# One of three gathered blocks' second-table rows weighed and added by GpSimd, and the gathers dealt out anew

## The chip, the cores and the metric

The kernel runs on one core of a Trainium2 chip. Its engines are TensorE (PE), VectorE (DVE), ScalarE (ACT), GpSimd (POOL) and SyncE (SP); each runs its own list of instructions in order and they meet only in semaphores. The metric is the device time of one execution in microseconds; a kernel's time is the median of its runs.

## The reference

One layer over 1024 positions of width 1024: an input projection, a gated mixer with a 128x128 spatial product, a short convolution, an output projection and layer norm. Then comes the part that the change touches, a product-key layer of single-neuron experts:

```python
q = (xb @ w_q).reshape(t, PEER_HEADS, 2, PEER_HALF)
s = jnp.einsum('thpd,hpkd->thpk', q, sub_keys)
# top 16 of each half, the sums' top 16: idx (16384 experts), gate = softmax
u = jnp.take(expert_u, idx, axis=0)
act = jax.nn.gelu(jnp.einsum('thkd,td->thk', u, xb))
v = jnp.take(expert_v, idx, axis=0)
return jnp.einsum('thk,thkd->td', gate * act, v)
```

Each of 1024 positions picks 8 x 16 = 128 experts of 16384, each with a row of 1024 values in either table.

## The kernel before

The eight blocks of 128 positions are treated in two ways. Blocks 0 to 2 ("A") gather: for each of 3 x 8 x 16 = 384 slots an indirect DMA brings the 128 positions' rows of `u_rows` (the first table), 128x1024 float32 or 0.52 MB, and a second one those of `v_rows`. Slot s belongs to block s % 3. Blocks 3 to 7 ("B") go through both whole tables as matrix products on TensorE, with activations spread from the gates.

The program's order is one list of units, each a weight block of 1 MB: the A units, then for B the kinds V, C, U, M, O, Q (query heads, 8), E (64 expert units of the first table), W (64 half units of the second table, in 32 groups). Query units 2 to 7 stand between the first expert units, one after each five. Most units need their weights split in a high and a low float16 part: `make_hi` on ScalarE (L697), `make_lo` on VectorE (L919), four units ahead, from two `stage` buffers. Expert units 0 to 39 lie beside VectorE's ranking of B's queries; the gates come beside unit 38 (L1334), and TensorE transposes ids and gates (L1737) before its unit 39 is followed by anything else. Units 40 to 59 are the spreading units, in which TensorE also multiplies one-hot tiles (L1721).

The gathers lie beside these units. `SECTION` says how many slots each unit takes, `_rows()` puts the unit's u rows (24 slots ahead) and then its v rows in the one list `ROWS` (768), and `_places()` gives each row a buffer of the ring that is free at that time: 8 buffers beside U and M ("front"), 4 beside O, Q and expert units 37 to 39 ("own"), 6 beside expert units 0 to 36 ("rank") and from 40 on ("spread"), 9 beside W ("out"). GpSimd issues all gathers in this order (L681); before each it waits until the row that last had the buffer is used (`row_used`, L680), and at the start of "out" until the last a_dram store has landed. VectorE uses the rows in the same order, in the midst of its other work: a u row is one dot product with `h2_sp` (L1022), a v row one scaled addition to `acc_sp` (L1031). ScalarE's first `coefficients_hi` waits for the last row in the buffers 10 and 11 (`SPREAD_ROWS`), SyncE's load of expert unit 0 for the last in the stage buffers (`FRONT_ROWS`). After the last group's `coefficients_lo` (L1503) SyncE loads what the closing layer norms need, and VectorE closes the eight blocks.

Of the kernel before, what the change touches and what calls it, by code (L numbers as in the profile page):

```python
# [43 lines left out]
SB = NBLK["A"]  # L44
# [172 lines left out]
ROWS = _rows()  # L217
ROW_OF = {row[:2]: m for m, row in enumerate(ROWS)}


# [28 lines left out]
PHASE = [_buffers_of(SEC_UNITS[c]) for _, _, c in ROWS]  # L249
FRONT_ROWS = max(m for m, (r, _, _) in enumerate(PLACES) if 4 <= r < 8) + 1  # L250
SPREAD_ROWS = max(m for m, (r, _, _) in enumerate(PLACES) if r in (10, 11)) + 1

# [10 lines left out]
def trunk_layer(nc, x, c_row, w_cond, b_col, w_front, ln_g, ln_b, w_spat, b_spat, conv_w,  # L263
                ln1_g, ln1_b, keys_t, u_units, v_units, u_rows, v_rows, ln2_g, ln2_b, out):
    with ExitStack() as ctx:
# [212 lines left out]
        acc_zeroed = sem("acc_zeroed")  # L478
        row_used = sem("row_used")
        gelu_ready = sem("gelu_ready")  # L480
        weight_ready = sem("weight_ready")
# [33 lines left out]
        def _(sp):  # L515
# [13 lines left out]
            def load(n):  # L529
                x, kind, u = UNITS[n]  # L530
                if CONVERTED[n]:
# [4 lines left out]
                    if (x, kind, u) in (("B", "E", 0), ("B", "E", 1)):  # L536
                        sp.wait_ge(row_used, FRONT_ROWS)
                    src = u_units[u] if kind == "E" else v_units[u] if kind == "W" else w_front[FRONT[kind] + u]
# [116 lines left out]
        def _(pool):  # L655
# [11 lines left out]
            pool.wait_ge(h2_ready, 1)  # L667
            pool.memset(acc_sp[:, :, :], 0.0).then_inc(acc_zeroed, 1)
            for m, (table, slot, _) in enumerate(ROWS):
# [9 lines left out]
                if before is not None:  # L679
                    pool.wait_ge(row_used, before + 1)  # L680
                pool.indirect_dma_start(row_at[r], None, u_rows if table == "u" else v_rows,  # L681
                                        bass.IndirectOffsetOnAxis(ap=idx_sp[:, slot:slot + 1], axis=0)
                                        ).then_inc(row_in[r], 16)

        @block.scalar
        def _(act):
# [42 lines left out]
            def gelu_dots(c):  # L729

                k = len(SEC_U[c])
                if k:
                    act.wait_ge(row_used, ROW_OF["u", SEC_U[c][-1]] + 1)
                    d = dots[:, c % 4, 0:k]
                    activation(d, d, ACT.Gelu_apprx_tanh).then_inc(gelu_ready, 1)
# [167 lines left out]
        def _(dve):  # L903
# [121 lines left out]
            def v_row(slot):  # L1025
                r, _, uses = PLACES[ROW_OF["v", slot]]
                dve.wait_ge(row_in[r], 16 * (uses + 1))
                if slot >= SB:
                    dve.wait_ge(row_used, ROW_OF["v", slot - SB] + 1)
                dst = acc_sp[:, slot % SB, :]  # L1030
# [16 lines left out]
            def section(unit):  # L1047
# [470 lines left out]
            for g in range(NGRP):  # L1518
# [20 lines left out]
                for _ in rest:  # L1539
                    pass  # L1540
            dve.wait_ge(row_used, len(ROWS))
            dve.wait_ge(end_in, 48)
# [270 lines left out]
```

## Time and profile before

| what | value |
|---|---|
| median of three runs | 3172.84 us (3171.23 to 3173.77) |
| the profiled execution's own time | 3179.19 us |
| its span, first to last instruction | 3177.4 us |
| mean granted TensorE clock | 0.965 |
| busy: TensorE, VectorE, ScalarE, GpSimd | 2923.4, 2580.6, 814.7, 1019.7 us |
| bytes moved by DMA | 917.51 MB, mean 289 GB/s |

A busy time counts an engine's instructions without waits. It is a sum over stages with different limits, so which engine sets the time is to be read stage by stage. Gather issues count as GpSimd's busy time.

### The profile page before, as it was taken

Reading aid. Unit: us, or ns where it says so; the run is one execution under the profiler, and the core shown is the slowest. Engines: PE = TensorE matmul, PEld = TensorE weight load, DVE = VectorE, ACT = ScalarE, POOL = GpSimd, SP = SyncE. Lnnn points to the kernel's source line nnn. Section 1 sums busy time; section 2 is a strip of 40 time slices with the busy share of each in tenths; the row PEclk is TensorE's granted clock in tenths of the full one; section 3 lists DMA queues with packets and bytes.
Section 4 is the critical chain, followed back from the end, with each engine's and each line's share of the span. In section 5 each row is a group of like instructions: output and inputs, shape, how many; then the busy total and the mean of one; then the engine's idle time right before and its main releaser. Section 6 shows DMA issues by size and latency. Waiting matters only on the chain.

```text
span 3177.4 us, 46997 instructions
## 1 busy us (share of the span) xinstructions
PE 2923.4 (92%) x19088; PEld 1919.1 (60%) x19088; DVE 2580.6 (81%) x4794; ACT 814.7 (26%) x1190; POOL 1019.7 (32%) x778
## 2 busy tenths in 40 slices
PE   4899979997899679999999799999799999999994
PEld 3556667776676556777777588888544444444442
DVE  6875656996676869999998787777589999999977
ACT  2333322211111222222222233333222222222220
POOL 0000000003554104544454511111356566656510
PEclk9999989999999889999999899999899999999997
DMA  9888543334898247988887878888899999999953
GB/s 353 308 311 316 215 161 134 140 106 171 297 357 328 86 181 261 328 314 313 295 327 284 303 257 263 261 264 269 326 388 410 408 413 408 412 413 409 406 231 126
DMA packets 266232, 917.51 MB, mean 289 GB/s; under 512 B 20464, under 2 KB 102432, under 8 KB 222752
## 3 DMA queue, kind: packets, MB, share of 16 engines
q1 hardware_dynamic: 63968, 427.91, 35.2%
q0 software_dynamic: 110592, 402.70, 33.7%
q10 hardware_dynamic: 91456, 83.89, 8.1%
q8 instruction: 151, 2.47, 0.3%
q14 instruction: 65, 0.53, 0.0%
HBM read 771.79 MB, written 142.63 MB: 288 GB/s over the span
## 4 chain that ended last, share of the span: by engine, by line
PE 82%; DVE 9%; DMA 4%; issue 2%; ACT 1%; POOL 1%; SPq 0%; DVEq 0%; ACTq 0%
PE psU L1590 21%; PE psU L1591 20%; PE psU L1592 20%; PE psX L1592 5%; PE psX L1590 5%; PE psX L1591 5%; PE psX L1721 5%; DMA rows<-in_v_rows,idx_sp 2%; PE psX L1659 1%; DVE w L919 1%; DVE stats L938 1%; DMA R<-in_x 1%; DVE acc_sp L1031 1%; POOL rows L681 0%; DMA Z<-mod_dram 0%
## 5 line engine op out<-in xcount | busy, mean ns | idle before, releaser
L1590 PE MATMUL psU<-hB,w 128*128 128x320 f16 x3072 | 924.8, 301 | 25.9 <-ACT R L688 13.8
L1592 PE MATMUL psU<-hB,w 128*128 128x320 f16 x3072 | 921.3, 300 | 2.2 <-issue 2.2
L1591 PE MATMUL psU<-hB,w 128*128 128x320 f16 x3072 | 921.4, 300 | 1.1 <-issue 1.1
L919 DVE SCALAR_TENSOR_TENSOR w<-stage,w 128x2048 f16<-128x2048 f32 x176 | 402.5, 2287 | 142.8 <-ACT w L688 142.6
L681 POOL DMA_INDIRECT rows<-in_u_rows,idx_sp x216 | 287.4, 1330 | 551.7 <-DVE rows L1022 494.3
L688 ACT ACTIVATE w<-stage 128x2048 f16<-128x2048 f32 x176 | 335.6, 1908 | 397.4 <-PE psX L1592 346.7
L1590 PEld LDWEIGHTS psU<-hB,w 128*128 128x128 f16 x3072 | 304.3, 99 | 140.8 <-issue 28.8
L1591 PEld LDWEIGHTS psU<-hB,w 128*128 128x128 f16 x3072 | 304.4, 99 | 115.5 <-issue 4.0
L1592 PEld LDWEIGHTS psU<-hB,w 128*128 128x128 f16 x3072 | 301.2, 98 | 119.8 <-issue 1.6
L681 POOL DMA_INDIRECT rows<-in_v_rows,idx_sp x218 | 280.1, 1285 | 244.4 <-DVE acc_sp L1031 111.8
L1590 PE MATMUL psX<-w,Z 128*128 128x512 f16 x768 | 292.0, 380 | 23.9 <-DVE Z L1514 23.9
L1590 PE MATMUL psU<-w,Z 128*128 128x512 f16 (+1 forms) x768 | 268.3, 349 | 41.7 <-DVE Z L1503 22.2
L1031 DVE SCALAR_TENSOR_TENSOR acc_sp<-rows,weight_sp,acc_sp 128x1024 f32<-128x1024 f32 x218 | 275.0, 1292 | 37.1 <-DMA rows<-in_v_rows,idx_sp 26.1
L1591 PE MATMUL psX<-w,Z 128*128 128x512 f16 x768 | 292.1, 380 | 0.0
L1592 PE MATMUL psX<-w,Z 128*128 128x512 f16 x768 | 292.1, 380 | 0.0
L1591 PE MATMUL psU<-w,Z 128*128 128x512 f16 (+1 forms) x768 | 268.0, 349 | 0.0
L1592 PE MATMUL psU<-w,Z 128*128 128x512 f16 (+1 forms) x768 | 267.7, 349 | 0.0
L1022 DVE SCALAR_TENSOR_TENSOR rows<-rows,h_sp 128x1024 f32<-128x1024 f32 x216 | 258.4, 1221 | 6.8 <-DMA rows<-in_u_rows,idx_sp 5.8
L688 ACT ACTIVATE Z<-psU 128x320 f32<-128x320 f32 (+1 forms) x224 | 100.5, 452 | 556.0 <-PE psU L1592 459.2
L688 ACT ACTIVATE R<-psU 128x320 f32<-128x320 f32 (+1 forms) x296 | 122.9, 427 | 368.1 <-PE psU L1592 337.5
L1590 PE MATMUL psU<-Z,w 128*128 128x384 f16 (+1 forms) x640 | 206.0, 322 | 0.0
L1592 PE MATMUL psU<-Z,w 128*128 128x384 f16 (+1 forms) x640 | 205.9, 322 | 0.0
(251 smaller groups left out, 4505.1 us busy)
## 6 DMA issues: line engine op xcount, KB each, us to landing
stage<-in_u_units SPq DMA_DIRECT2D x64, 1024.0 KB
stage<-in_v_units SPq DMA_DIRECT2D x64, 1024.0 KB
stage<-in_w_front SPq DMA_DIRECT2D x48, 1024.0 KB
hl_dram<-w SPq DMA_DIRECT2D x48, 1024.0 KB, 5.6
w<-hl_dram SPq DMA_DIRECT2D x48, 1024.0 KB, 4.9
a_dram<-R ACTq DMA_DIRECT2D x64, 640.0 KB
g_dram<-Z ACTq DMA_DIRECT2D x20, 2048.0 KB, 15.6
Z<-a_dram SPq DMA_DIRECT2D x32, 1280.0 KB, 11.8
```

What stands on the lines that cost most here:

```text
L681: pool.indirect_dma_start(row_at[r], None, u_rows if table == "u" else v_rows, bass.IndirectOffsetOnAxis(ap=idx_sp[:, slot:slot + 1], axis ...
L688: return nc.scalar.activation(dst, src, func, scale=scale)
L919: V.scalar_tensor_tensor(w[:, n % NW, 1, :], stage[:, v % 2, :], WS, w[:, n % NW, 0, :], ALU.mult, ALU.subtract).then_inc(lo_done, 1)
L938: step(V.bn_stats(stats[:, b, half, :], src[:, b - first, half * HT:(half + 1) * HT]))
L1022: V.scalar_tensor_tensor(row_at[r], row_at[r], 1.0, h2_sp[:, slot % SB, :], ALU.mult, ALU.mult, accum_out=dots[:, c % 4, j:j + 1]).then_in ...
L1031: V.scalar_tensor_tensor(dst, row_at[r], weight_sp[:, slot:slot + 1], dst, ALU.mult, ALU.add).then_inc(row_used, 1)
L1590: mm(ps, lhs[0](k), rhs[0](k), start=start and s == 0, stop=False)
L1591: mm(ps, lhs[0](k), rhs[1](k), start=False, stop=False)
L1592: last = mm(ps, lhs[1](k), rhs[0](k), start=False, stop=stop and s == n - 1)
L1659: ins = mm(ps[:, m * P:(m + 1) * P], qb[:, half, b * P:(b + 1) * P], keys[:, 2 * h + half, :], start=True, stop=True)
L1721: ins = mm(ps[:, t * P:(t + 1) * P], oh_keys[:, q % 4, 0, :, t], oh_gate[:, q % 4, c, :, t], start=(c == 0), stop=(c == 1))
```

## The change

GpSimd weighs and adds the v rows of block 2 (`BY_POOL`: slot % 3 == 2), 128 of 384, in two instructions: `tensor_scalar` with the slot's weight in place in the row's buffer, a wait for its own semaphore, and `tensor_tensor` into `acc_sp`. It does so between its gather issues: before it issues row m it has added its rows up to m - 5, and up to the row that last had the buffer of row m. `row_used` counts VectorE's rows alone, `pool_used` GpSimd's, and whoever waited for `row_used` now waits for one or both. `SECTION` gives each expert unit three slots and each spreading unit two, where it was two or three and one or two; the W groups take the rest, 144 slots for 174. The rows of each ring become: rank 222 (184 before), own 58 (56), spread 104 (84), out 264 (324), front 120 as before.

```diff
-        k["B", "E", e] = 2 + e % 2 if e < E_SPREAD else 1 + e % 2 if e < E_SPREAD + N_SPREAD else 3
+        k["B", "E", e] = 2 if E_SPREAD <= e < E_SPREAD + N_SPREAD else 3
...
+BY_POOL = [table == "v" and slot % SB == SB - 1 for table, slot, _ in ROWS]
+POOL_USED = [sum(BY_POOL[:m + 1]) for m in range(len(ROWS))]
+ROWS_USED = [m + 1 - POOL_USED[m] for m in range(len(ROWS))]
+POOL_LEAD = 5
...
+            def add_row(m):
+
+                _, slot, c = ROWS[m]
+                r, _, uses = PLACES[m]
+                pool.wait_ge(row_in[r], 16 * (uses + 1))
+                pool.wait_ge(weight_ready, WEIGHED[slot])
+                if slot >= SB:
+                    pool.wait_ge(pool_used, POOL_USED[m] - 1)
+                dst = acc_sp[:, slot % SB, :]
+                pool.tensor_scalar(row_at[r], row_at[r], weight_sp[:, slot:slot + 1], None, ALU.mult).then_inc(row_weighed, 1)
+                pool.wait_ge(row_weighed, POOL_USED[m])
+                pool.tensor_tensor(dst, row_at[r], dst, ALU.add).then_inc(pool_used, 1)
...
+                while added <= m - POOL_LEAD or before is not None and added <= before:
+                    if BY_POOL[added]:
+                        add_row(added)
+                    added += 1
...
-                    pool.wait_ge(row_used, before + 1)
+                    pool.wait_ge(row_used, ROWS_USED[before])
+                    if POOL_USED[before]:
+                        pool.wait_ge(pool_used, POOL_USED[before])
...
-                    act.wait_ge(row_used, SPREAD_ROWS)
+                    act.wait_ge(row_used, ROWS_USED[SPREAD_ROWS])
+                    act.wait_ge(pool_used, POOL_USED[SPREAD_ROWS])
...
                 for slot in SEC_V[c]:
-                    v_row(slot)
-                    yield
+                    if not BY_POOL[ROW_OF["v", slot]]:
+                        v_row(slot)
+                        yield
...
+            dve.wait_ge(pool_used, POOL_USED[-1])
```

## Rows read from the trace of the kernel before

**Rows 1.** The page's tenths: busy share in 40 equal slices.

```profile
PE   4899979997899679999999799999799999999994
DVE  6875656996676869999998787777589999999977
POOL 0000000003554104544454511111356566656510
```

**Rows 2.** Windows: us, then busy of PE, PEld, DVE, ACT, POOL, clock, DMA share, GB/s.

```profile
850.00:1000.00 150.00, 149.01 (x1095) 106.78 (x1093) 100.12 (x125) 21.16 (x57) 72.64 (x67) 1.00 0.86 330
...
1268.00:1670.00 402.00, 402.00 (x2979) 292.73 (x2979) 373.11 (x1046) 106.83 (x190) 200.68 (x150) 1.00 0.87 315
...
1850.00:2200.00 350.00, 350.00 (x2723) 288.09 (x2721) 278.38 (x382) 132.54 (x238) 57.11 (x51) 1.00 0.82 264
...
2400.00:3000.00 600.00, 600.00 (x2781) 272.01 (x2780) 586.03 (x647) 142.40 (x92) 368.76 (x260) 1.00 1.02 410
```

**Rows 3.** The chain (start us, us, what): two query heads' scores, one period apart.

```profile
1267.75 2.23 PE psX L1659 x20
1348.22 2.23 PE psX L1659 x20
```

**Rows 4.** Waits in 1268 to 1670 us: us in total, times, longest.

```profile
POOL Z L681 <- DVE Z L1022: 90.6, 8, 20.5
POOL rows L681 <- DVE rows L1022: 72.7, 20, 7.8
```

**Rows 5.** VectorE's timeline about 1691 to 1697 us: start us, us.

```profile
1691.22 1.22 DVE L1022 SCALAR_TENSOR_TENSOR Z<-Z,h_sp 128x1024 f32<-128x1024 f32 x1
...
1692.37 2.48 DVE L1031 SCALAR_TENSOR_TENSOR acc_sp<-rows,weight_sp,acc_sp 128x1024 f32<-128x1024 f32 x2
...
1694.83 2.28 DVE L919 SCALAR_TENSOR_TENSOR w<-stage,w 128x2048 f16<-128x2048 f32 x1
```

**Rows 6.** GpSimd's timeline in the same stretch.

```profile
1691.57 1.68 POOL L681 DMA_INDIRECT Z<-in_u_rows,idx_sp  x1 [18.90 <-DVE Z L1022]
1693.56 0.94 POOL L681 DMA_INDIRECT Z<-in_v_rows,idx_sp  x1 [0.31 <-issue]
1694.80 3.13 POOL L681 DMA_INDIRECT rows<-in_v_rows,idx_sp  x1 [0.30 <-issue]
```

**Rows 7.** Groups by line: GpSimd's instructions that are no gathers.

```profile
L668 POOL MEMSET acc_sp<- 128x3072 f32 x1 | 2.7, 2664 | 296.3 <-issue 296.3
L663 POOL MEMSET Z<- 64x512 f32 x2 | 1.0, 520 | 460.9 <-DMA Z<-in_w_spat 460.9
L658 POOL TENSOR_SCALAR_AFFINE_SELECT ident<-ident 128x128 f32<-128x128 f32 x1 | 0.3, 285 | 0.2 <-POOL ident L656 0.2
...
L656 POOL MEMSET ident<- 128x128 f32 x1 | 0.2, 206 | 0.3 <-POOLq L1806 0.3
```

**Rows 8.** The chain ahead of the gates, and TensorE's waits in 1640 to 1830.

```profile
1748.33 13.40 DMA rows<-in_v_rows,idx_sp
...
1776.63 9.26 DMA rows<-in_v_rows,idx_sp
```

```profile
PE psX L1737 <- DVE Z L1334: 14.9, 1, 14.9
PE psX L1737 <- DVE Z L1359: 3.5, 1, 3.5
PE psX L1721 <- DVE Z L1383: 2.8, 1, 2.8
```

**Rows 9.** The chain and GpSimd's timeline between spreading and W groups.

```profile
2280.57 2.93 DMA a_dram<-R
...
2283.95 9.61 DMA Z<-g_dram
...
2296.72 2.35 ACT Z L688
```

```profile
2284.28 0.94 POOL L681 DMA_INDIRECT R<-in_u_rows,idx_sp  x1 [14.41 <-DMA a_dram<-R]
```

**Rows 10.** VectorE's timeline and the chain at the end.

```profile
3094.52 0.69 DVE L1514 TENSOR_TENSOR Z<-psX,Z 128x512 f32<-128x512 f32 x1 [1.75 <-PE psX L1592]
```

```profile
3095.13 2.83 DVE Z L1503
...
3102.93 12.05 DMA Z<-in_ln_b
```

More of the change, by code:

```diff
@@ L218 @@
 ROW_OF = {row[:2]: m for m, row in enumerate(ROWS)}
+BY_POOL = [table == "v" and slot % SB == SB - 1 for table, slot, _ in ROWS]
+POOL_USED = [sum(BY_POOL[:m + 1]) for m in range(len(ROWS))]
+ROWS_USED = [m + 1 - POOL_USED[m] for m in range(len(ROWS))]
+POOL_LEAD = 5
+WEIGHED = [sum(1 for c in range(len(SEC_U)) if SEC_U[c] and SEC_U[c][0] <= slot) for slot in range(SLOTS)]
 BUFFERS = {"front": [0, 1, 2, 3, 4, 5, 6, 7], "own": [0, 1, 2, 3], "rank": [0, 1, 2, 3, 8, 9],
@@ L249 @@
 PHASE = [_buffers_of(SEC_UNITS[c]) for _, _, c in ROWS]
-FRONT_ROWS = max(m for m, (r, _, _) in enumerate(PLACES) if 4 <= r < 8) + 1
-SPREAD_ROWS = max(m for m, (r, _, _) in enumerate(PLACES) if r in (10, 11)) + 1
+FRONT_ROWS = max(m for m, (r, _, _) in enumerate(PLACES) if 4 <= r < 8)
+SPREAD_ROWS = max(m for m, (r, _, _) in enumerate(PLACES) if r in (10, 11))
 SHARED = ((1, 0), (4, 0), (2, 1))
@@ L479, in trunk_layer @@
         row_used = sem("row_used")
+        pool_used = sem("pool_used")
+        row_weighed = sem("row_weighed")
         gelu_ready = sem("gelu_ready")
@@ L536, in load @@
                     if (x, kind, u) in (("B", "E", 0), ("B", "E", 1)):
-                        sp.wait_ge(row_used, FRONT_ROWS)
+                        sp.wait_ge(row_used, ROWS_USED[FRONT_ROWS])
+                        sp.wait_ge(pool_used, POOL_USED[FRONT_ROWS])
                     src = u_units[u] if kind == "E" else v_units[u] if kind == "W" else w_front[FRONT[kind] + u]
@@ L668, in _ @@
             pool.memset(acc_sp[:, :, :], 0.0).then_inc(acc_zeroed, 1)
+            def add_row(m):
[9 more added lines that the diff above has]
+                pool.tensor_tensor(dst, row_at[r], dst, ALU.add).then_inc(pool_used, 1)
+            pool.wait_ge(acc_zeroed, 1)
+            added = 0
             for m, (table, slot, _) in enumerate(ROWS):
                 r, before, _ = PLACES[m]
+                while added <= m - POOL_LEAD or before is not None and added <= before:
+                    if BY_POOL[added]:
+                        add_row(added)
+                    added += 1
                 if m and PHASE[m] != PHASE[m - 1]:
@@ L683, in _ @@
                                         ).then_inc(row_in[r], 16)
+            for m in range(added, len(ROWS)):
+                if BY_POOL[m]:
+                    add_row(m)
         @block.scalar
@@ L732, in gelu_dots @@
                 if k:
-                    act.wait_ge(row_used, ROW_OF["u", SEC_U[c][-1]] + 1)
+                    act.wait_ge(row_used, ROWS_USED[ROW_OF["u", SEC_U[c][-1]]])
                     d = dots[:, c % 4, 0:k]
@@ L1028, in v_row @@
                 if slot >= SB:
-                    dve.wait_ge(row_used, ROW_OF["v", slot - SB] + 1)
+                    dve.wait_ge(row_used, ROWS_USED[ROW_OF["v", slot - SB]])
                 dst = acc_sp[:, slot % SB, :]
@@ L1540, in _ @@
                     pass
-            dve.wait_ge(row_used, len(ROWS))
+            dve.wait_ge(row_used, ROWS_USED[-1])
+            dve.wait_ge(pool_used, POOL_USED[-1])
             dve.wait_ge(end_in, 48)
```

## The prediction

> **What bounds the kernel now.** I read the page's tenths first, then stages by window, then who waits for whom, then the chain where TensorE is not full. In the tenths TensorE's row is nearly all nines from the middle of the span on, while VectorE's row is as high and GpSimd's stands at 4 to 6 [rows 1]. The windows make it exact. From 1268 to 1670 us (expert units beside ranking) TensorE is busy for all 402 us, VectorE for 373.11 (93%), GpSimd for 200.68. From 1850 to 2200 (spreading units) TensorE is full again, VectorE at 80%, GpSimd at 16%. From 2400 to 3000 (the W groups) TensorE is full, VectorE at 98%, DMA at its ceiling of 410 GB/s, GpSimd at 61% [rows 2]. In all three the granted clock is 1.00, the 2.4 GHz level [rows 2], so no work taken from VectorE there shortens them. That is the first thing to see: the most loaded helper, VectorE in the W groups, does not set the end.
>
> What is left to win or lose is where TensorE waits. One place is just before the spreading: TensorE waits 14.90 us for VectorE's gates (L1334), and on the chain ahead of it stand landings of second-table rows, 13.40 and 9.26 us, with four row buffers [rows 8]. Another is 2280 to 2302, set by the store of a_dram, the load of g_dram and the first coefficients [rows 9]. The end is the last: coefficients_lo(31) starts at 3095.13 right behind a VectorE instruction that had waited 1.75 us for TensorE, and 12.05 us of parameter loads follow [rows 10]. TensorE sets that start, not the rows, so relief in the W groups does not move the end.
>
> **The change, part by part.** (1) It moves 128 of 384 v rows from VectorE to GpSimd: 16 beside the M units, 37 + 9 + 18 beside ranking, its four-buffer units and spreading, 48 in the W groups. (2) It moves 30 slots (60 gathers) out of the W groups into expert units; a ranking unit now always has 3. (3) GpSimd adds rows in its own order, before it issues the gather five places later, and before it reuses that buffer. So behind an add on its queue stand all further gathers, and VectorE waits for those.
>
> VectorE, ranking stage. TensorE takes 80.47 us for five expert units and one query unit, from one score group to the next but same [rows 3]. VectorE works 373.11/5 = 74.6 us of that. Its slots per such period go from 14.5 to 17: 2.5 more u rows at 1.15 us (1691.22 to 1692.37) is +2.9; v rows on VectorE go from 14.5 to 11.33, 3.17 fewer at 1.20 us, -3.8 [rows 5]. It ends at 73.7: the relief is eaten by the added slots.
>
> VectorE, W groups. 30 u rows and 78 v rows fewer over 31 groups is (34.5 + 93.6)/31 = 4.1 us less per 25.6 us. Value: 0, since TensorE is full [rows 2]. If anything were late there, the cover is now 4.7 us per group instead of 0.6.
>
> GpSimd, one row. No row shows a two-input operation on GpSimd. From below: its memset writes 3072 columns in 2664 ns and 512 in 520, 0.84 ns per column and 0.09 fixed, so two passes over 1024 columns can't take under 1.9 us. The nearest row with a read is the affine select, 285 ns for 128 columns, about 1.5 ns per column or 1.6 us for 1024 [rows 7]; I take that for the multiply. For the add, one further read at the memset's 0.84: 2.3 ns per column, 2.5 us. Between the two and before the first a semaphore hand-over of 0.2 or 0.3 [rows 7]. I take 1.6 + 2.5 + 0.5 = 4.6 us. From above: 3.1 us for the add (twice the one-read rate) and, for each of the two, half of the 2.2 us that a gather issue stood still beside L919 (3.13 against 0.94) [rows 5, 6]: 7.4 us.
>
> The Trainium skill, "GPSIMD Engine Reference", section 3.1, has 4497 ns for an fp32 tensor_tensor of 2048 columns. By it the add would be some 2.25 us, an estimate, and the sum of one row 4.35; this case's trace of before has no such instruction.
>
> GpSimd, ranking stage. A gather issue costs 200.68/150 = 1.34 us busy [rows 2] and 0.30 behind it [rows 6], 1.64. Now 34 per period: 55.7 us. Adds: 17/3 = 5.67 at 4.6: 26.1. Together 81.8 us, against 80.47: the engine that had spare time has none. It also can't use all of its time. Today it waits 90.6 us in 8 waits (11.3 each) and 72.7 in 20 for u rows to be used [rows 4]; the long ones come while VectorE sorts, with all six buffers full. An add (4.6) fits into each long wait and 6.7 remains, 1.6 times per period: 10.7 us. VectorE, once late, comes back to rows that are ready, so I count half, 5.4. Period 87.2, +6.8. There are 37 expert units with the ring of six, 7.4 periods: +50 us. With 1.9 us for a row it is 55.7 + 10.8 + 10.7 = 77.2, under 80.47: +0. With 7.4: 55.7 + 42.0 + 5.4 = 103, +22.6, 167 us.
>
> Does VectorE's lateness reach TensorE? make_lo runs four units ahead, so for up to three units (some 40 us) TensorE would not see it. But gates("B") has no such lead: TensorE stands there already today for 14.90 us [rows 8]. What lateness has piled up by then comes out in full at that place. The cover is borrowed, not kept.
>
> The four-buffer units (37 to 39). A GpSimd row in a ring of four must land and be added before its buffer is issued again. Landing is 9 to 13 us there [rows 8]; one add of 4.6 stands in front of the rows that VectorE awaits before the gates: +5 (0 to 10).
>
> M units. 72.64/67 + 0.30 = 1.38 per issue, six are 8.3, with an add 12.9, beside units of about 13.1 us (96 of 1095 products in 150 us). VectorE is busy for only 100 of 150 us there [rows 2], so small lags are hidden: 0. With 7.4 us per row it would be +2.6 x 16 = 42 at most.
>
> Spreading. GpSimd at 16% and VectorE at 80% take +0.5 u row and 0.67 add per unit: 0 [rows 2]. Transition: the last spreading row (slot 239, buffer 11) is now GpSimd's and comes behind the wait for a_dram and four issues: 2284.28 + 5.0 + 4.6 = 2293.9, and coefficients_hi(0), which now waits for it, starts at 2296.72 [rows 9]. Cover 2.8 us: 0, or +4 from above. DMA: 60 gathers of 0.52 MB come in at 315 GB/s and leave at 410 [rows 2]: 0 by itself.
>
> Sum: 50 + 5 = +55. The profiled execution took 3179.19 us (span 3177.4 and 1.8 around it), so 3234.2. That execution is 6.35 over the median of the three runs, so the median should be 3172.84 + 55 = 3228.
>
> **Rivals.** (a) *GpSimd bounds the gathers of the ranking stage*: the forecast, +15 to +120, chance 0.50.
>
> (b) *GpSimd's reads hold VectorE*. The trace has a hold in the one direction: an issue of 3.13 us beside L919, though 0.94 beside L1031 [rows 5, 6], and u and v rows keep 1.22 and 1.24 us beside issues. If each GpSimd pass held VectorE for all its 4.1 us, VectorE would need 73.7 + 23.2 = 96.9 per period, +16.4, 121 us in 7.4 periods, and in the W groups 25.0 - 4.1 + 6.3 = 27.2 against 25.6, +50. If VectorE wants the port half the time: 85.3, +4.8, 36 us, and nothing in the W groups. I take the middle of 36 and 121, +78, 3250. Chance 0.22.
> The Trainium skill says this, "SBUF — State Buffer": a VectorE instruction with two SBUF inputs and a GpSimd instruction that reads SBUF exclude each other for the whole instruction. By that rule (b) is the outcome; the trace agrees for L919 beside an issue and shows nothing for L1031.
>
> (c) *It fits* (a row at 2 to 3 us): within 6 us of 3173. For it: GpSimd's 200 idle us of 402. Against it: the six buffers. Chance 0.19.
>
> (d) *Faster*: v rows off VectorE shorten what stands before the gates. Today landings fill that chain and VectorE waits at v rows [rows 8]; if GpSimd takes over one such wait per unit and its row costs under 2.5 us (the two VectorE v rows of 1.24 us that follow it in a unit), up to the 14.90 us and the 6.3 behind it go. From there it decides: -12, 3161. Against it: the rows issued behind it wait for the same landing. Chance 0.09.
>
> **How the numbers follow.** The likeliest is (a): 3228. A measurement of this kernel tells about 0.2%, 6.3 us, from no change. Faster 0.09 is (d); same is (c) and the foot of (a), 0.20; slower 0.71. The range starts at 3167, the low edge of (c), and leaves (d) out; up to 3295 it takes (a) to +120 and most of (b), leaving some 0.1 above.
>
> **What would show it.** In the changed profile: the two GpSimd groups x128, their means (1.6 and 2.5 us); GpSimd near full in the ranking stage with VectorE waiting for row landings or GpSimd; a longer wait for L1334, over 14.90; W groups still full at 25.6 us; the tail unchanged. Holds would show as L1022, L919 or L1031 longer or late. I am wrong if a row costs under 3 us and VectorE's lateness before the gates does not grow.

## The result, and the profile after

The changed kernel takes 3450.65 us (median of four runs, 3444.14 to 3454.92) where the kernel before took 3173.31 beside it: a ratio of 1.0871 [1.0848, 1.0894], or +277 us. The forecast was +55, with 3295 as the upper end. The direction came true; the size is five times the forecast and outside the range.

The page of the changed kernel: busy sums, the tenths of three engines, and the shares of the chain that ended last.

```profile
PE 2983.3 (87%) x19088; PEld 1935.1 (56%) x19088; DVE 2698.6 (78%) x4665; ACT 801.9 (23%) x1189; POOL 1828.1 (53%) x1034
...
PE   3999979989986778888987499999699999999995
...
DVE  6866549967667688888898689998588878888877
...
POOL 0000000018884167777887764344677887888870
...
PE 37%; POOL 27%; issue 16%; DMA 11%; DVE 7%; ACT 0%; SPq 0%; POOLq 0%; DVEq 0%
```

Against [rows 1] TensorE has sevens and eights (and one nine) in slices 16 to 22, in the ranking stage and behind it, where it had nines throughout, and GpSimd has risen to sevens and eights in most slices with gathers, though only to threes and fours in the spreading stage (slices 25 to 28). Two sums look wrong at first. VectorE gave up 128 rows (some 160 us) and is busy 118 us longer. TensorE has the same 19088 instructions and is busy 60 us longer.

Windows of the changed kernel (columns as in [rows 2]), placed in the same stages: M units, ranking, spreading, W groups.

```profile
850.00:1000.00 150.00, 142.04 (x1021) 100.91 (x1020) 99.95 (x102) 19.24 (x54) 129.51 (x76) 0.98 0.79 283
1268.00:1670.00 402.00, 343.40 (x2395) 241.28 (x2394) 340.98 (x845) 79.83 (x153) 312.27 (x184) 0.92 0.77 275
2010.00:2360.00 350.00, 350.00 (x2723) 288.14 (x2721) 323.09 (x401) 132.23 (x238) 153.05 (x96) 1.00 0.88 289
2600.00:3200.00 600.00, 556.75 (x2476) 245.56 (x2475) 498.18 (x482) 126.54 (x82) 497.79 (x256) 0.96 0.85 328
```

Against [rows 2], only spreading is still full. In ranking TensorE ran 2395 products in 402 us where it had run 2979, and the granted clock is 0.92 for 1.00: it has pauses now, and the products behind them run at a lower clock. 343.40/2395 is 143 ns for a product, against 135 before; in the W groups it is 225 ns for 216. That is where TensorE's 60 extra us come from. Its idle time grew by 205 us, and the two together are the 265 us by which the span grew (3177.4 to 3442.3). In the W groups VectorE fell from 98% to 83%, and TensorE stalls there all the same, with the DMAs at 328 GB/s instead of 410. The 83% match the forecast by chance: they are 23.3 us of a group that now takes 28.1, where I had reckoned 20.9 of 25.6.

The stages, cut at the first and last score group, the first transposes behind the gates, and the first and last `coefficients_lo`, in us of the span; two experiments stand beside for later use:

| stage | before | after | deal alone (e1) | GpSimd adds in W only (e7) |
|---|---|---|---|---|
| up to the first scores | 1153.3 | 1175.9 | 1148.2 | 1150.3 |
| ranking | 518.7 | 619.4 | 544.3 | 544.2 |
| to the transposes behind the gates | 119.6 | 169.1 | 136.3 | 136.4 |
| spreading and transition | 507.6 | 524.3 | 511.4 | 511.5 |
| W groups | 795.9 | 871.5 | 795.3 | 867.1 |
| end | 82.3 | 82.1 | 82.9 | 82.8 |

Groups of the changed kernel by line (columns as in [rows 7]; L1058, L1067, L955, L1531 are before's L1022, L1031, L919, L1494):

```profile
L955 DVE SCALAR_TENSOR_TENSOR w<-stage,w 128x2048 f16<-128x2048 f32 x176 | 428.6, 2436 | 128.8 <-ACT w L723 128.6
L1058 DVE SCALAR_TENSOR_TENSOR rows<-rows,h_sp 128x1024 f32<-128x1024 f32 x194 | 258.0, 1342 | 68.5 <-DMA rows<-in_u_rows,idx_sp 68.0
L689 POOL TENSOR_SCALAR rows<-rows,weight_sp 128x1024 f32<-128x1024 f32 x86 | 254.8, 2963 | 46.4 <-DMA rows<-in_v_rows,idx_sp 43.6
L691 POOL TENSOR_TENSOR acc_sp<-rows,acc_sp 128x1024 f32<-128x1024 f32 x86 | 244.3, 2841 | 7.2
L1067 DVE SCALAR_TENSOR_TENSOR acc_sp<-rows,weight_sp,acc_sp 128x1024 f32<-128x1024 f32 x170 | 242.0, 1437 | 138.8 <-DMA rows<-in_v_rows,idx_sp 70.8 <-issue 67.5
...
L1531 DVE SCALAR_TENSOR_TENSOR Z<-Z 128x640 f32<-128x640 f32 x128 | 129.1, 1069 | 12.9 <-DMA Z<-g_dram 12.9
```

One GpSimd row is 2.96 + 2.84 us, with two small gaps (below) 5.8 to 6.0, where I had put 4.6. It is inside my bounds of 1.9 to 7.4, but the multiply, which I took for the cheap pass at 1.6, is the dear one. The second reading is on VectorE: L1058 has 1342 ns for some 1220 and L955 2436 for 2280 [rows 5]. Over whole lines, VectorE's busy time above what the same number of instructions took before is 48 us at L1058, 50 at L1067, 26 at L955, 33 at L1531, and 42 at L1080, which multiplies two or three columns. The two-input operations of the spreading stage add 26 (L1420) and 13 (L1413). These seven lines hold 238 of the 278 us that are to be explained. Idle time behind landing gathers has come too, 68.0 and 70.8 us in these groups.

How the reads hold the other engine can be read instruction by instruction. GpSimd, then VectorE, in the timeline of the changed kernel:

```profile
1269.90 2.71 POOL L691 TENSOR_TENSOR acc_sp<-rows,acc_sp 128x1024 f32<-128x1024 f32 x1
...
1283.16 2.86 POOL L689 TENSOR_SCALAR rows<-rows,weight_sp 128x1024 f32<-128x1024 f32 x1
1286.10 2.35 POOL L691 TENSOR_TENSOR acc_sp<-rows,acc_sp 128x1024 f32<-128x1024 f32 x1
1288.61 1.82 POOL L713 DMA_INDIRECT rows<-in_u_rows,idx_sp  x1 [0.15 <-POOL acc_sp L691]
```

```profile
1270.33 2.31 DVE L1080 SCALAR_TENSOR_TENSOR weight_sp<-dots,gate_sp 128x3 f32<-128x3 f32 x1
...
1286.18 3.36 DVE L1067 SCALAR_TENSOR_TENSOR acc_sp<-rows,weight_sp,acc_sp 128x1024 f32<-128x1024 f32 x1 [0.39 <-DMA rows<-in_v_rows,idx_sp]
1289.46 0.15 DVE L1080 SCALAR_TENSOR_TENSOR weight_sp<-dots,gate_sp 128x3 f32<-128x3 f32 x1
1289.54 2.28 DVE L955 SCALAR_TENSOR_TENSOR w<-stage,w 128x2048 f16<-128x2048 f32 x1
```

The add ends at 1288.45. The v row that VectorE began 0.08 us behind the add's start ends at 1289.54, which is 1.09 us after the add's end: it waited for the whole add and ran then. Three columns at L1080 take 0.15 us when alone and 2.31 at 1270.33, up to 1272.64, where the add ends at 1272.61. The other direction, GpSimd first:

```profile
1357.80 3.75 POOL L691 TENSOR_TENSOR acc_sp<-rows,acc_sp 128x1024 f32<-128x1024 f32 x1
...
1404.34 4.13 POOL L689 TENSOR_SCALAR rows<-rows,weight_sp 128x1024 f32<-128x1024 f32 x1
```

```profile
1357.05 2.28 DVE L955 SCALAR_TENSOR_TENSOR w<-stage,w 128x2048 f16<-128x2048 f32 x1
...
1403.47 2.29 DVE L955 SCALAR_TENSOR_TENSOR w<-stage,w 128x2048 f16<-128x2048 f32 x1
1406.04 1.77 DVE L1058 SCALAR_TENSOR_TENSOR rows<-rows,h_sp 128x1024 f32<-128x1024 f32 x1 [0.29 <-DMA rows<-in_u_rows,idx_sp]
```

Both GpSimd passes are longer by what was left of L955 when they began. The last line adds a refinement. The multiply got going at about 1405.6 (its end, 1408.47, less 2.86); a u row started at 1406.04 beside it took 0.55 us too long, not the 2.4 that were left. The add holds VectorE for all its time, the multiply for about its first microsecond. This is not one pair's accident. In the whole trace 16 of VectorE's two-input instructions (L1058, L1067, L955) began within 0.25 us of a multiply's getting going, and were 0.84 us too long in the median; the 83 that began a microsecond or more behind it were not longer at all. All 48 that began beside an add with over 0.3 us of it left were too long by what was left less 0.13 to 0.20 us.

TensorE's waits between 1250 and 1990 us, changed kernel (columns as the second fence of [rows 8]):

```profile
PE psU L1628 <- ACT R L723: 89.8, 19, 10.7
PE psX L1775 <- DVE Z L1371: 31.2, 1, 31.2
PE psX L1775 <- DVE Z L1396: 12.4, 1, 12.4
```

The wait at the gates went from 14.9 to 31.2 us, the one behind it from 3.5 to 12.4, and before the gates there are 89.8 us in 19 waits (and 10.3 in 6 for ScalarE's copy into Z) that [rows 2] had none of. None of these waits is for `make_lo`. The longest of the ranking stage, TensorE, ScalarE and VectorE:

```profile
1327.19 0.30 PE L1630 MATMUL psU<-hB,w 128*128 128x320 f16 x1
1337.88 0.43 PE L1628 MATMUL psU<-hB,w 128*128 128x320 f16 x1 [10.39 <-ACT R L723]
```

```profile
1337.21 0.20 ACT L723 ACTIVATE dots<-dots 128x3 f32<-128x3 f32 x1 [22.08 <-DVE rows L1058]
1337.32 1.40 ACT L723 ACTIVATE R<-psU 128x320 f32<-128x320 f32 x4
```

```profile
1335.94 1.22 DVE L1058 SCALAR_TENSOR_TENSOR rows<-rows,h_sp 128x1024 f32<-128x1024 f32 x1
```

TensorE waits until ScalarE has copied its results out of the four `psU` tiles. ScalarE's list has, in each unit, the copies of this unit and then the gelu over the dot products of the unit before (`section_gelu`), and that gelu waits until VectorE has used the last u row of that unit. Behind it stand the next unit's copies. So VectorE's lateness at a u row stops ScalarE first and then TensorE. From the first scores of this stage to the gates TensorE has 27 waits, 114.2 us, and in every one the copy that it waits for stands right behind such a gelu; at the 21 that fall to expert units the unit's own low half had been ready for 22 to 53 us. Before there were 2 such waits, with 13.8 us. ScalarE's waits at the gelu between 1268 and 1670 us went from 73.5 to 305.0 us. The kernel before had them already:

```profile
ACT dots L688 <- DVE rows L1022: 40.8, 12, 8.6
ACT dots L688 <- DVE Z L1022: 32.7, 10, 6.6
```

There, from 1254 to 1698 us, the gelu ended only 3.6 to 12.7 us before TensorE began its next unit. That was the cover in ranking, and not the units by which `make_lo` is ahead.

Behind a pause the products also come more slowly. Ahead of this one they start 0.135 us apart, behind it 0.266, about the ratio of the clock's two levels, 2.4 and 1.2 GHz.

Which engine holds the W groups shows in GpSimd's waits from 2600 to 3200, changed kernel:

```profile
POOL rows L689 <- DMA rows<-in_v_rows,idx_sp: 30.7, 10, 5.6
POOL R L713 <- issue: 26.8, 88, 0.3
POOL rows L713 <- issue: 17.7, 58, 0.3
POOL R L689 <- DMA R<-in_v_rows,idx_sp: 14.1, 6, 4.0
```

497.8 us busy, 44.5 of gaps between issues and 44.8 in which it stands at a row not yet landed make 587 of 600: GpSimd never waits for VectorE or a buffer worth naming. It sets 871.5/31 = 28.1 us for a group that TensorE would do in 25.6. VectorE waits for the landings, and TensorE for VectorE: 49.8 us in 17 waits, all at L1551, where VectorE takes over TensorE's sums.

### The profile page after: what moved, and what is told of

The parts are those of the page before. It is cut to its first block, busy times and chain, and to the rows that moved or that the text cites. A ratio compares the mean times of both kernels' runs of the same rounds, so it can differ in the third digit from the quotient of the medians.

```text
span 3442.3 us, 47841 instructions
## 1 busy us (share of the span) xinstructions
PE 2983.3 (87%) x19088; PEld 1935.1 (56%) x19088; DVE 2698.6 (78%) x4665; ACT 801.9 (23%) x1189; POOL 1828.1 (53%) x1034
## 4 chain that ended last, share of the span: by engine, by line
PE 37%; POOL 27%; issue 16%; DMA 11%; DVE 7%; ACT 0%; SPq 0%; POOLq 0%; DVEq 0%
PE psU L1628 10%; PE psU L1629 10%; PE psU L1630 10%; POOL rows L713 8%; POOL acc_sp L691 7%; POOL rows L689 5%; DMA rows<-in_v_rows,idx_sp 5%; PE psX L1759 4%; DMA R<-in_v_rows,idx_sp 3%; POOL R L713 3%; POOL Z L713 2%; POOL R L689 2%; PE psX L1628 1%; PE psX L1629 1%; PE psX L1630 1%
## 5 line engine op out<-in xcount | busy, mean ns | idle before, releaser
L1628 PE MATMUL psU<-hB,w 128*128 128x320 f16 x3072 | 940.2, 306 | 133.0 <-ACT R L723 104.0
L1629 PE MATMUL psU<-hB,w 128*128 128x320 f16 x3072 | 936.8, 305 | 0.0
L1630 PE MATMUL psU<-hB,w 128*128 128x320 f16 x3072 | 936.3, 305 | 0.0
L955 DVE SCALAR_TENSOR_TENSOR w<-stage,w 128x2048 f16<-128x2048 f32 x176 | 428.6, 2436 | 128.8 <-ACT w L723 128.6
L1628 PEld LDWEIGHTS psU<-hB,w 128*128 128x128 f16 x3072 | 308.8, 101 | 260.2 <-issue 141.9
L713 POOL DMA_INDIRECT rows<-in_v_rows,idx_sp x256 | 334.0, 1305 | 177.6 <-DVE rows L1058 110.3
L713 POOL DMA_INDIRECT rows<-in_u_rows,idx_sp x194 | 266.9, 1376 | 265.0 <-DVE rows L1058 143.2
L1630 PEld LDWEIGHTS psU<-hB,w 128*128 128x128 f16 x3072 | 305.8, 100 | 125.8
L1629 PEld LDWEIGHTS psU<-hB,w 128*128 128x128 f16 x3072 | 308.6, 100 | 117.8
L1628 PE MATMUL psX<-w,Z 128*128 128x512 f16 x768 | 300.1, 391 | 73.7 <-DVE Z L1551 73.6
L1067 DVE SCALAR_TENSOR_TENSOR acc_sp<-rows,weight_sp,acc_sp 128x1024 f32<-128x1024 f32 x170 | 242.0, 1437 | 138.8 <-DMA rows<-in_v_rows,idx_sp 70.8
L1058 DVE SCALAR_TENSOR_TENSOR rows<-rows,h_sp 128x1024 f32<-128x1024 f32 x194 | 258.0, 1342 | 68.5 <-DMA rows<-in_u_rows,idx_sp 68.0
L1629 PE MATMUL psX<-w,Z 128*128 128x512 f16 x768 | 300.4, 391 | 0.0
L1630 PE MATMUL psX<-w,Z 128*128 128x512 f16 x768 | 300.4, 391 | 0.0
L689 POOL TENSOR_SCALAR rows<-rows,weight_sp 128x1024 f32<-128x1024 f32 x86 | 254.8, 2963 | 46.4 <-DMA rows<-in_v_rows,idx_sp 43.6
L691 POOL TENSOR_TENSOR acc_sp<-rows,acc_sp 128x1024 f32<-128x1024 f32 x86 | 244.3, 2841 | 7.2
## 6 DMA issues: line engine op xcount, KB each, us to landing
Z<-a_dram SPq DMA_DIRECT2D x32, 1280.0 KB, 10.3
```

The lines of the kernel that those rows point to most:

```text
L689: pool.tensor_scalar(row_at[r], row_at[r], weight_sp[:, slot:slot + 1], None, ALU.mult).then_inc(row_weighed, 1)
L691: pool.tensor_tensor(dst, row_at[r], dst, ALU.add).then_inc(pool_used, 1)
L955: V.scalar_tensor_tensor(w[:, n % NW, 1, :], stage[:, v % 2, :], WS, w[:, n % NW, 0, :], ALU.mult, ALU.subtract).then_inc(lo_done, 1)
L1058: V.scalar_tensor_tensor(row_at[r], row_at[r], 1.0, h2_sp[:, slot % SB, :], ALU.mult, ALU.mult, accum_out=dots[:, c % 4, j:j + 1]).then_in ...
L1067: V.scalar_tensor_tensor(dst, row_at[r], weight_sp[:, slot:slot + 1], dst, ALU.mult, ALU.add).then_inc(row_used, 1)
L1628: mm(ps, lhs[0](k), rhs[0](k), start=start and s == 0, stop=False)
```

## The experiments

Each ratio is to the kernel before, run beside it (3168 to 3176 us); "after" is the changed kernel.

**The parts separated.** e1 takes the new deal of slots alone; e2 the GpSimd rows with the old deal; e3 the whole change with GpSimd's passes on 8 of 1024 columns. In e3 the other 1016 columns of block 2's rows are neither weighed nor added.

```diff
# e1, from before
-        k["B", "E", e] = 2 + e % 2 if e < E_SPREAD else 1 + e % 2 if e < E_SPREAD + N_SPREAD else 3
+        k["B", "E", e] = 2 if E_SPREAD <= e < E_SPREAD + N_SPREAD else 3
# e2, from after: the same line put back
# e3, from after
-                pool.tensor_scalar(row_at[r], row_at[r], weight_sp[:, slot:slot + 1], None, ALU.mult)...
+                pool.tensor_scalar(row_at[r][:, 0:8], row_at[r][:, 0:8], weight_sp[:, slot:slot + 1], None, ALU.mult)...
-                pool.tensor_tensor(dst, row_at[r], dst, ALU.add)...
+                pool.tensor_tensor(dst[:, 0:8], row_at[r][:, 0:8], dst[:, 0:8], ALU.add)...
```

> The new deal of slots alone (three beside each expert unit, two beside each spreading unit), all v rows on VectorE as before. Theory Q (GpSimd's in-order queue: two passes of 2.86 and about 2.6 us per row stand before all further gathers): the deal costs little by itself, 3160 to 3195 us, ranking stage at 80.5 to 82 us per period. Theory D (the deal is what costs, because 30 slots more lie beside ranking, where VectorE already worked 74.6 of 80.47 us): VectorE needs 74.6 + 2.5 x 1.15 + 2.5 x 1.20 = 80.5 us per period, the gates come late, 3200 us or more.

> GpSimd's adds as in the changed kernel, the old deal of slots. Theory Q: the same 128 rows cost the same queue time, but with 29 instead of 34 gathers per ranking period and 5.6 instead of 4.65 slots per W group, so the loss moves from the ranking stage to the W groups: 3380 to 3480 us in all. Theory D: near the kernel before, under 3230 us.

> As the changed kernel, but GpSimd weighs and adds only 8 of the 1024 columns of each of its rows (the other columns of block 2's sum are left out). Every wait and its place in the queue stays; the passes shrink from about 5.6 us to some 0.4 us. Theory Q (time of the passes, and what they hold): back to 3175 to 3215 us. Rival L (the wait for a row's landing only five rows after its issue is what costs): 3350 us or more, since that wait is unchanged.

Measured: e1 3221.33 us, 1.0152 [1.0134, 1.0169]; e2 3501.59, 1.1034 [1.1014, 1.1054]; e3 3224.41, 1.0154 [1.0135, 1.0173].

e1 is the first miss: I had valued the deal at nothing, and it costs 48 us without one GpSimd row. e2 came out dearer than its range (3480 at most), e3 a little above its own (3215). The chain of e1 in the ranking stage (start us, us, what):

```profile
1293.16 1.68 POOL Z L681
...
1297.63 7.21 DMA rows<-in_v_rows,idx_sp
...
1307.14 2.56 DVE acc_sp L1031 x2
...
1309.78 2.24 DVE w L919
...
1324.90 11.17 DMA rows<-in_v_rows,idx_sp
```

Three slots are six rows, and the ring there has six buffers. A unit's first gather can go out only when VectorE has used the row of the unit before, so every unit runs issue, landing (7.21, then 11.17 us), row, `make_lo`, in one chain. With two slots in every other unit, GpSimd could get ahead. TensorE's 41.3 us of waits from the first scores to the gates of e1, 9 of them, again all stand behind a gelu of dot products. There is a rival: in e1 all v rows are VectorE's, and its sum for a period is 74.6 + 2.9 + 3.0 = 80.5 us of 80.47. e3 speaks against it. There VectorE has a third of the v rows less (73.7 us) and is busy for 86% of the ranking stage instead of e1's 94%, yet the stage takes 546.7 us for 544.3. So I take the landings to set it, and the engines' sums can't show this.

e3 equals e1: the waits, the order and the changed semaphores are free at this size, and a row whose two passes are short (means near 1.0 and 0.7 us) hides entirely. So the pass time and the reads cost the rest, 228 us. e2 shows that the deal's price is not additive: with the adds the new deal saves 51 us. In e2 58 GpSimd rows and 324 gathers lie beside the W groups, which take 1025 us; after has 48 and 264, and 871.5. Where GpSimd is the bound, taking gathers away from it pays.

**Queue time or reads?** e5 leaves the weighing and adding of block 2's rows out and puts five awaited memsets of 1024 columns in their place: as long in GpSimd's queue, but without a read. e6 leaves out the weighing, e9 the adding.

```diff
# e5, from after
-                pool.tensor_scalar(...).then_inc(row_weighed, 1)
-                pool.wait_ge(row_weighed, POOL_USED[m])
-                pool.tensor_tensor(...).then_inc(pool_used, 1)
+                for i in range(4):
+                    pool.memset(row_at[r], 0.0).then_inc(row_weighed, 1)
+                    pool.wait_ge(row_weighed, 4 * (POOL_USED[m] - 1) + i + 1)
+                pool.memset(row_at[r], 0.0).then_inc(pool_used, 1)
# e6: the tensor_scalar and the wait behind it are gone
# e9: the tensor_tensor is gone, the tensor_scalar counts in pool_used
```

> As the changed kernel, but in place of the multiply and the add GpSimd sets the landed row to zero five times, each memset awaited (block 2's sum is left out). Queue time per row stays at about 5.5 us (5 x (0.95 + 0.15)), but GpSimd reads nothing from SBUF. Theory Q (the time in GpSimd's queue is what costs, 226 us over the run with thin adds): near the changed kernel, 3400 to 3450 us. Rival H (GpSimd's reads and VectorE's two-input instructions hold each other; VectorE's row and split groups are some 190 us longer in the changed kernel than their counts explain): 3300 us or less, with the means of the row groups and of make_lo back at 1.22, 1.29 and 2.29 us.

> As the changed kernel, but GpSimd adds its rows without weighing them (block 2's weights on the GpSimd rows are left out), so one pass of some 2.6 us per row instead of two of 5.5 together. If the cost is proportional to the time of the passes: 3224 + 226 x 0.47 = 3330 us. Theory Q says less, since GpSimd then fits: 34 x 1.64 + 5.67 x 2.8 = 71.6 of 80.47 us per ranking period, and 15.6 + 1.55 x 2.8 = 20 of 25.6 us per W group: 3240 to 3290 us, with the W groups (first to last coefficients_lo) at 796 to 810 us instead of 871.

> As the changed kernel, but GpSimd only weighs its rows and never adds them (block 2's GpSimd rows are left out of the sum): one pass of 2.86 us, a little longer in the queue than the add of 2.35 to 2.7. In the changed kernel's trace an add holds a VectorE instruction with two inputs until its own end, the weighing only for about its first microsecond. If holds decide: less than the 3258 us of the run without weighing, 3230 to 3250. If queue time alone decides: as much or more, 3258 to 3275 us.

Measured: e5 3320.84 us, 1.0448 [1.0427, 1.0469]; e6 3257.58, 1.0265 [1.0244, 1.0286]; e9 3249.06, 1.0265 [1.0249, 1.0281]. Groups of e5 (its L956, L1059, L1068 are after's L955, L1058, L1067):

```profile
L956 DVE SCALAR_TENSOR_TENSOR w<-stage,w 128x2048 f16<-128x2048 f32 x176 | 402.6, 2288 | 144.1 <-ACT w L724 143.7
L690 POOL MEMSET rows<- 128x1024 f32 x344 | 330.4, 960 | 81.0 <-DMA rows<-in_v_rows,idx_sp 64.5 <-issue 1.6
L1059 DVE SCALAR_TENSOR_TENSOR rows<-rows,h_sp 128x1024 f32<-128x1024 f32 x194 | 234.9, 1222 | 99.2 <-DMA rows<-in_u_rows,idx_sp 81.4 <-issue 17.1
L1068 DVE SCALAR_TENSOR_TENSOR acc_sp<-rows,weight_sp,acc_sp 128x1024 f32<-128x1024 f32 x170 | 216.0, 1284 | 142.7 <-issue 78.7 <-DMA rows<-in_v_rows,idx_sp 63.1
```

VectorE's means are back at 2288, 1222 and 1284 ns: without reads nothing is held. What is left is a row of 5.0 us in the queue, and it costs 2.9% (1.0448 less 1.0154, about 93 us); VectorE then waits for landings, 81.4 us at u rows and 63.1 at v rows. The real passes cost a further 4.2% (1.0871 less 1.0448, about 134 us). That step holds two things: VectorE held by the reads, and a row that is itself some 0.8 to 1.0 us longer than e5's. About 0.4 of this is the passes' own length (5.4 us unhindered against 5.0), the rest is GpSimd held by VectorE. e5's 3321 us are above the 3300 that went with the holds as the cause and far below the 3400 that went with queue time: neither is all of it.

By stage, in us of the span, as in the table above:

| stage | e3 | e6 | e9 | e5 |
|---|---|---|---|---|
| up to the first scores | 1147.7 | 1147.2 | 1147.2 | 1159.5 |
| ranking | 546.7 | 568.1 | 561.5 | 579.5 |
| to the transposes behind the gates | 137.7 | 147.4 | 144.8 | 149.8 |
| spreading and transition | 511.3 | 514.9 | 514.6 | 518.6 |
| W groups | 795.3 | 795.1 | 796.3 | 832.9 |

Beside W a single pass is free, whichever it is. e6's adds keep VectorE busy there for 707 us where e3's keep it for 630, and yet the groups take no more time. So in the W groups holds on VectorE cost nothing by themselves, and what costs is GpSimd's queue. The real passes fill that queue further, 702 us busy against 603 in e5. Of what the real passes cost over e5, some 39 us lie in the W groups, 40 in ranking, 19 ahead of the gates, 16 in and before the M units and 6 in spreading.

e6 and e9 were meant to tell which pass does the harm, and do not. The add holds VectorE far more (e6's v rows have a mean of 1637 ns, e9's 1388), the multiply alone is longer (3.16 us against 2.64), and both cost the same, 1.1% or 35 us over the deal. Two such halves make 70, the whole makes 228. Costs don't add because GpSimd has slack: 34 issues of 1.64 us leave 25 us of an 80.47 us period, one pass of 3 us takes 17 of them, two of 5.8 take 33 and are over. For the W groups the table bears this out. For ranking it is only worked out from sums, and it is not the whole: single passes cost 21 and 15 us there over e3, though they fit by the sum. The points are, in the order e3, e6, e9, e5 and after, rows of about 1.9, 2.9, 3.4, 5.0 and 5.9 us, and costs of +0, +35, +35, +93 and +228 us.

**Where in the kernel?** e7 lets GpSimd add only slots from 240 on, those beside the W groups. e10 lets it add a row eight places behind its issue instead of five.

```diff
# e7, from after
-BY_POOL = [table == "v" and slot % SB == SB - 1 for table, slot, _ in ROWS]
+BY_POOL = [table == "v" and slot % SB == SB - 1 and slot >= 240 for table, slot, _ in ROWS]
# e10, from after
-POOL_LEAD = 5
+POOL_LEAD = 8
```

> The new deal, and GpSimd adds only its 48 rows beside the W groups; the other 80 stay on VectorE. If stages add up: 3221 us of the deal alone plus the 76 us that the W groups grew in the changed kernel, 3297 us. If the loss in the W groups were only lateness carried in from the ranking stage: 3225 us, W groups at 796 us.

> The changed kernel with GpSimd's rows added eight places behind the issues instead of five (it bites in the rings of eight and nine; smaller rings force the add earlier). GpSimd waited 78 us for landings in front of its weighing. If these waits cost: the M units and the W groups gain, some 30 us in all, 3420 us. If passes and holds are the cost: within 10 us of 3450, since the engine only does the same work later.

Measured: e7 3294.99 us, 1.0382 [1.0365, 1.04]; e10 3410.67, 1.077 [1.0754, 1.0786]. e7's stages stand in the table above: everything up to the W groups is e1's, the W groups are the changed kernel's (867.1 and 871.5). So the W loss is made in the W groups and is not inherited. The windows of e7, ranking and W:

```profile
1268.00:1670.00 402.00, 385.93 (x2793) 277.12 (x2792) 375.10 (x1047) 95.87 (x177) 202.03 (x161) 0.98 0.88 321
2600.00:3100.00 500.00, 461.64 (x2064) 203.86 (x2062) 411.69 (x401) 104.60 (x68) 413.00 (x214) 0.96 0.85 329
```

e10 takes away nearly all of GpSimd's standing at rows not landed (73.7 us in after, 2.2 in e10) and gives back 1%; W goes from 871.5 to 836.2 us, ranking stays (632.9 for 619.4). The lead of five was part of the W loss, not the main part of the whole.

**Is it the ring of six, and what do the slots want?** e12 is the kernel before with the same number of slots moved out of W, but all 30 to the spreading units (three each); ranking is untouched. e8 goes the other way: the kernel before with fewer slots ahead of the gates. e11 and e13 are e8 with SyncE's first loads of coefficients taken up ahead of the W groups' weight loads: both groups', or the first alone.

```diff
# e12, from before
+        k["B", "E", e] = 2 + e % 2 if e < E_SPREAD else 3
# e8, from before
+        k["B", "E", e] = (1 if e in (36, 37, 38) else 2 + e % 2) if e < E_SPREAD else (2 if e < E_SPREAD + 8 else 1 + e % 2) if e < E_SPREAD + N_SPREAD else 3
# e13, on top of e8 (e11: load_group(1) follows load_group(0) here too)
             for n in range(n_o + 4, first_w + 4):
+                if n == first_w:
+                    for b in range(2):
+                        sp.wait_ge(g_stored[b], 16 * N_SPREAD // 2)
+                    for r in range(4):
+                        sp.wait_ge(a_stored[r], 16)
+                    load_group(0)
                 load(n)
...
-            load_group(0)
```

> The kernel before, its 30 slots taken out of the W groups as in the change, but all given to the spreading units (three each), none to the units beside ranking; nothing on GpSimd but gathers. If the 48 us of the new deal come from six rows per unit in ranking's ring of six buffers (no row in flight for the next unit, so VectorE awaits a landing): 3173 to 3185 us, first to last query scores back at 519 us, the spreading (gates to first coefficients_lo) up from 508 us by some microseconds since VectorE's spare 4 us per unit are taken. If it is the smaller load of the W groups or the moved slots as such: 3200 us or more.

> The kernel before with another deal: one slot beside each of the expert units 36 to 38, just ahead of the gates, and two beside four spreading units that had one; nothing on GpSimd but gathers. If row landings in the ring of four are what makes the gates late (14.9 us of TensorE's waiting): 3155 to 3168 us. If VectorE's own work sets the gates: 3173 us, no change.

> The kernel before with the deal of the light-gates run, and SyncE issues the loads of the first two W groups (a_dram, g_dram) ahead of the weight loads of the first four W units, as soon as the spreading's stores have landed, instead of after the last a_dram store. The 22 us between the last expert unit and the first W product hold 2.9 us of store and 9.6 us of load. If that is what they are: first coefficients_lo some 12 us earlier, 3151 us. If the weight loads, now behind them, come late instead: no gain, 3163 us or more.

> As the early-groups run, but only the first W group's two loads go ahead of the W weight loads; the second group's stay behind. In that run a weight load that took 24.11 us to land behind four group loads ate the gain. With half of the bytes ahead: W's first coefficients_lo at 2270 to 2276 us of the span instead of 2280 (light gates) and 2285 (both early), 3152 to 3158 us. If any load ahead of the weights costs what it gives: 3163 us again.

Measured: e12 3174.78 us, 1.0015 [1.0006, 1.0024]; e8 3163.17, 0.9964 [0.9951, 0.9978]; e11 3165.64, 0.9987 [0.9978, 0.9996]; e13 3156.99, 0.9955 [0.9942, 0.9969].

e12 shows that what costs in e1 is not the load taken from W but its place: as many gathers cost 0.15% when they go to the spreading units, and 1.52% when they go to ranking, and the ranking stage is back at 518.1 us. That it is the ring there, rests on e1's chain and on e3; ranking with more than six buffers was not run. TensorE's waits from 1740 to 2320 in e13, whose lines stand two further down (L1739 is L1737, L1505 is L1503):

```profile
PE psU L1592 <- DVE Z L1505: 9.6, 1, 9.6
PE psX L1739 <- DVE Z L1336: 6.7, 1, 6.7
```

The gates wait fell from 14.9 [rows 8] to 6.7 with four slots fewer in units 36 to 38: the rows had made the gates late by those 8 us. The wait for the first coefficients fell from 22.2 in before to 9.6. The gate part and the first loads each give less than the waits promise, since other waits follow (5.0 for ScalarE). In e11, which loses what e13 wins, a weight load stands behind two groups' loads; the same one takes 17.54 us in e13:

```profile
2222.56 24.11 DMA stage<-in_v_units
```

e13 beats both kernels, by 0.45% and 8.5%. Beside e8 its interval overlaps, so what the early load adds is not shown as a time, only as a shorter wait.

## Why the prediction was right or wrong

The sum was +50 for ranking, +5 for the units ahead of the gates and 0 for all else. By the stages of the span it is +100.7 for ranking, +49.5 from there to the transposes behind the gates, +22.6 up to the first scores, +16.7 for spreading and transition, +75.6 for the W groups and -0.2 for the end.

**What bounds the kernel now: right.** Work taken off VectorE in a full stage brought nothing. In e3 VectorE is busy for 79% of the W groups instead of 94% before, and they take 795.3 us for 795.9.

**The deal of slots: wrong, the first failed step.** I costed (2) by engine sums ("the relief is eaten by the added slots", then 80.47 against 55.7 us) and got 0. It is +48 us, of which the span shows 26 in ranking and 17 ahead of the gates. The gathers of every unit now equal the ring, and landing time came onto the path (the chain of e1). The 90.6 us of long waits at full buffers [rows 4] were in my text, and I used them only to place the adds.

**The row of 4.6 us: mis-sized.** Unhindered it is 2.86 + 0.08 + 2.35 + 0.15 = 5.4; with the holds 5.8 to 6.0. The multiply was wrong by 1.3 us, since I took the affine select for it; the add at 2.35 was close to my 2.5. The estimate of 2.25 us for the add was half of the 4497 ns for 2048 columns in the Trainium skill's "GPSIMD Engine Reference", section 3.1, and 2.34 was the least measured: there it agrees, to 4%.

**W groups valued at 0: wrong, +76 us.** I gave them a cover of 4.7 us on VectorE and never made GpSimd's sum. With my own terms it would have been, for a group, 264/31 = 8.5 gathers at 1.64 and 48/31 = 1.55 rows at 4.6: 21.1 of 25.6 us, or 82%. Measured: issues 1.64 us long for 1.41 and 0.30 behind each (16.5), rows at 5.84 (9.0), which is 25.6 and full before any wait, and 2.1 of landings on top: 27.7 of the 28.1. A sum at 82% with landings of 9 to 13 us beside it was no cover to count on; the Value-0 line rested on the wrong engine.

**M units valued at 0: wrong, about +23 us** up to the first scores. GpSimd is at 86% there; the 42 that I named as the upper end was the right bound.

**How lateness reaches TensorE: wrong, the second failed step, and the one on the path.** I wrote that `make_lo` runs four units ahead, "so for up to three units (some 40 us) TensorE would not see it", and let all lateness come out at the gates. TensorE saw it by another way, ScalarE's gelu of the dot products, which stands ahead of the copies of TensorE's results: 27 waits, 114.2 us, before the gates. The cover there was 3.6 us at its least, not 40. I had followed one lead and not looked for the shortest one. At the gates the wait did grow, 14.9 to 31.2 us, as forecast.

**Rivals (a) and (b) as alternatives: the third failed step.** In the W groups (a) is at work, with GpSimd full. In ranking the engine is not near full, as (a) wanted it: busy for 456 of 619 us, with 44 between its issues, and for 104 it waits there for VectorE's u rows. Beside such a GpSimd VectorE is held, and I read it so that each makes the other dearer: a held VectorE uses rows later, which keeps buffers, which delays issues behind an add. No run shows this loop by itself. (a) alone is e5, +93 over the deal; the real passes bring the other 134. I gave each a price and a chance and never their joint price. The Trainium skill's rule in "SBUF — State Buffer", section "SBUF: two separate sides", that a VectorE instruction with two SBUF inputs and a GpSimd instruction reading SBUF exclude each other for the whole instruction, was the one to weigh higher: for the add the trace agrees (3.36 us for a v row of 1.24); for the multiply it shows a hold of only about 1 us of 2.86, and there the measurement decides.

**Spreading, transition and end: near enough**, +17, of which I had allowed 4, and -0.2.

**The clock: not in the sum at all.** TensorE's pauses lowered its granted clock to 0.92 in ranking and 0.96 in W, and the same products took 60 us more. I priced stalls as idle time only.

**(c) and (d):** e3 shows that (c) would have held for a row of some 1.9 us, on top of the deal's 48. At 2.9 us, still within its condition, the row costs 35 us (e6). (d) had a true core, since rows ahead of the gates are worth 0.36% (e8), but GpSimd was no way to get it.

**Open:** how the part of the 134 us that lies outside the W groups, some 81 us of the span, splits between VectorE held and GpSimd held; what a larger ring in ranking would give; and what the kernel would take with the gelu and its wait moved away from the copies. No run tried the last two.

## What to carry to other kernels

Before work goes to an engine that issues gathers, make that engine's own sum in every stage where it gets any, with issue, hand-over and landing waits, and count on no more cover than was measured. Here GpSimd's work and gaps for the W groups were free at 591 of 796 us, or 74% (e6), and cost 37 us at 668, or 84% (e5), with landings to wait for. When an engine gets late, follow every engine that waits for it to the one that sets the time: the shortest cover counts, here 3.6 us at ScalarE's gelu and not the four units of `make_lo`. Compare the number of transfers of one unit with the number of buffers: at equality there is no running ahead, and the landing time stands in every unit, also where the engines' sums leave room. Moving the few rows that stand before a serial point (here four slots ahead of the gates) was worth more than moving a third of the work to another engine.

## What the runs showed of the hardware

- A GpSimd multiply by a per-partition scalar, 128x1024 float32 in place, takes 2.84 us at least, more than the add of two tensors of that size (2.34); a memset of that size takes 0.95.
- The GpSimd add and VectorE's two-input instructions exclude each other for the whole instruction, in both directions and whatever the size: three columns took 2.31 us for 0.15. The multiply held a two-input instruction for about its first 1.0 us only (0.84 us in the median of 16 that began with it, nothing for 83 that began a microsecond later), but was itself held by L955 to its end (4.13 us).
- A gather issue is also prolonged beside L955 (2.95 us for 0.95 at 1272.77), as before [rows 6], and beside a two-input float16 `tensor_tensor` (1.89 us at 1276.03); beside W their mean rose from 1.41 to 1.64 us.
- On 8 columns GpSimd's two passes still take about 1.0 and 0.7 us in the mean (e3).
- Behind a pause of TensorE of 10.39 us products that had started 0.135 us apart started 0.266 apart; over the kernel 205 us more of pauses went with 60 us more of busy time for the same 19088 products.
